# Bias rows moved in four pieces, first units multiplied by their high parts first, and the latent columns made in two lanes, in a two-block transformer kernel

## The reference, cut to what matters

```python
z = h @ w_in                                  # first block; h = rmsnorm(x, g[0])
bias = jnp.transpose(rel_bias_table[bucket], (2, 0, 1))        # one row of distances per head, 12 heads
scores = jnp.where(valid, scores + bias[None, None, :, None], NEG_INF)
...
proj = jnp.einsum('bsd,de->bse', h, w_in[l])  # second block
ya = swa_attention(...)                       # 8 heads, sliding window
yb = mla_attention(...)                       # 4 heads; q and kv from latent columns:
#   q  = rmsnorm_2(c_q)  @ w_uq               (384 -> 4 x (128 + 64))
#   kv = rmsnorm_2(c_kv) @ w_ukv              (256 -> 4 x (128 + 128))
yc = diff_attention(...)                      # 4 heads of two softmaxes; out = rmsnorm_2(out, subln_g) * (1 - lam_init)
x = x + jnp.einsum('bse,ed->bsd', y, w_out[l])
```

## Time and profile before

| | us |
|---|---|
| median of 3 runs (2353.87 to 2355.01) | 2354.45 |
| the profiled execution, its own time | 2355.84 |
| its span, from the first to the last instruction | 2354.1 |
| PE busy | 2253.3 (96%) |
| DVE busy | 1362.3 (58%) |
| ACT busy | 1067.9 (45%) |
| mean granted clock of TensorE | 0.979 of 2.4 GHz |

### The profile page before, as it was taken

One profiled execution on the slowest core, in us unless ns is written; L12 is line 12 of the kernel. 1 busy time (PEld: TensorE's weight loads), 2 busy tenths in 40 slices (PEclk: granted clock), 3 DMA queues, 4 the chain that ended last, 5 costly groups with the idle time before them and its releaser, 6 DMA issues.

```text
span 2354.1 us, 31707 instructions
## 1 busy us (share of the span) xinstructions
PE 2253.3 (96%) x12978; PEld 1959.9 (83%) x12978; DVE 1362.3 (58%) x1718; ACT 1067.9 (45%) x1376; POOL 62.9 (3%) x66
## 2 busy tenths in 40 slices
PE   8799999888989999999999999999999999999998
PEld 7788898787877888888888888888986889889776
DVE  5446666566556666767666444655445555544554
ACT  5343542424455544544555334545435443544443
POOL 0000101002000000000000000000000000000000
PEclk9899999899989999999999999999999999999999
DMA  7756440014634555555565555553550556445143
GB/s 279 189 191 202 163 158 1 1 32 154 203 118 134 190 185 188 186 187 187 186 206 191 190 192 196 185 195 120 181 178 19 180 178 222 159 152 174 59 129 140
DMA packets 237804, 375.59 MB, mean 160 GB/s; under 512 B 8535, under 2 KB 110072, under 8 KB 236920
## 3 DMA queue, kind: packets, MB, share of 16 engines
q1 hardware_dynamic: 229596, 362.83, 46.3%
q10 hardware_dynamic: 8092, 11.11, 1.9%
HBM read 369.45 MB, written 4.46 MB: 159 GB/s over the span
## 4 chain that ended last, share of the span: by engine, by line
PE 65%; issue 5%; DVE 4%; ACT 2%; POOL 0%; DVEq 0%; POOLq 0%; ACTq 0%
PE PS L482 16%; PE PS L441 12%; PE PS L443 12%; PE PS L442 12%; PE PS L485 8%; DVE w_lo L359 1%; PE PS L2062 1%; ACT w_hi L354 1%; PE PS L2152 1%; PE PS L2136 1%; PE PS L2046 1%; PE PS L2827 1%; DVE h_both L938 0%; PE PS L921 0%; ACT spare L2074 0%
## 5 line engine op out<-in xcount | busy, mean ns | idle before, releaser
L359 DVE TENSOR_TENSOR w_lo<-raw,w_hi 128x2048 fp32r<-128x2048 f32 (+2 forms) x340 | 766.8, 2256 | 765.2 <-ACT w_hi L354 765.0
L354 ACT ACTIVATE w_hi<-raw 128x2048 fp32r<-128x2048 f32 (+2 forms) x340 | 641.2, 1886 | 876.0 <-PE PS L443 494.4
L482 PE MATMUL PS<-h_both,w_hi 128*128 128x512 f32 x1968 | 541.6, 397 | 12.2 <-DVE w_lo L359 9.4
L441 PE MATMUL PS<-w_hi,h_both 128*128 128x512 f32 (+2 forms) x1344 | 514.9, 383 | 11.7 <-DVE h_both L943 4.5
L442 PE MATMUL PS<-w_lo,h_both 128*128 128x512 f32 (+2 forms) x1344 | 507.2, 377 | 0.0
L443 PE MATMUL PS<-w_hi,h_both 128*128 128x512 f32 (+2 forms) x1088 | 408.3, 375 | 0.0
L482 PEld LDWEIGHTS PS<-h_both,w_hi 128*128 128x128 f32 x1968 | 338.1, 190 | 59.4 <-ACT arena L609 9.6
L485 PEld LDWEIGHTS PS<-h_both,w_lo 128*128 128x128 f32 x1968 | 303.2, 189 | 42.2
L485 PE MATMUL PS<-h_both,w_lo 128*128 128x256 f32 x1968 | 314.0, 281 | 0.0
L441 PEld LDWEIGHTS PS<-w_hi,h_both 128*128 128x128 f32 x1344 | 254.3, 189 | 60.0 <-issue 6.0
L442 PEld LDWEIGHTS PS<-w_lo,h_both 128*128 128x128 f32 x1344 | 254.6, 189 | 45.4
(11 more groups left out here) (569 smaller groups left out, 2003.4 us busy)
## 6 DMA issues: line engine op xcount, KB each, us to landing
raw<-in_w_in SPq DMA_DIRECT2D x132, 1024.0 KB, 5.0
raw<-in_ffn_w_up SPq DMA_DIRECT2D x176, 512.0 KB, 4.3
raw<-in_w_out SPq DMA_DIRECT2D x48, 1024.0 KB, 5.1
raw<-in_ffn_w_down SPq DMA_DIRECT2D x44, 1024.0 KB, 5.0
raw<-in_mem_wkv SPq DMA_DIRECT2D x8, 1024.0 KB, 11.5
raw<-in_mem_wq SPq DMA_DIRECT2D x4, 1024.0 KB, 5.1
raw<-in_mem_wo SPq DMA_DIRECT2D x4, 1024.0 KB, 7.2
raw<-in_w_in SPq DMA_DIRECT2D x4, 768.0 KB, 4.6
```

The costliest lines, as they stand in the source:

```text
L354: act.activation(w_hi[:, slot % 2, :st.n], raw[:, slot, :st.n], ACT.Copy).then_inc(hi_made, 1)
L359: dve.tensor_tensor(w_lo[:, slot % 2, :st.n], raw[:, slot, :st.n], w_hi[:, slot % 2, :st.n].bitcast(F32), ALU.subtract).then_inc(lo_made, 1)
L441: pe.matmul(ps, l_hi, r_hi, start=start, stop=False, skip_group_check=skip)
L482: pe.matmul(sums, wh[:, k, cs], h_both[:, :, kk, :], start=kk == 0, stop=False, skip_group_check=True)
```

## The change

It has six edits. (1) `opening_tensor` turns two pairs, then multiplies unit 0 by a new function: block by block the products with `h_hi`, with pairs 2 and 3 turned in between, and then all the products with `h_lo`. ST_MEM_K keeps the old way. In the wide stages, unit 0 is then made of matmuls of 256 columns. (2) In the `unscaled_` openings, unit 1 of the weights is split ahead of pairs 2 and 3. (3) The bias rows go out in four pieces of three heads, after ST_C's units 0, 3, 6 and 9, and come back in four pieces beside the stages after ST_CE; no wait stands between ST_BC and ST_C. (4) The latent columns are two jobs of 7 rounds, on lanes 2 and 3; `mla` heads 2 and 3 idle for 7 rounds. (5) `mixed_scalar` splits `w_out_2`'s unit 0 three rounds earlier. (6) `mixed_vector` does its part of that ahead of `diff_rows`, a round earlier.

```diff
+        def multiply_highs_first(pe, q, hi_ready, lo_ready, turn):
...
+            pe.wait_ge(lo_made, q.unit(1))
...
+            for k in range(st.kb):
+                hi_ready(k)
+                for o, ts, ns, first in rows:
+                    pe.matmul(o, h_hi[:, k, ts], wh[:, k, ns], start=k == 0 and first, stop=False, skip_group_check=True)
+                    pe.matmul(o, h_hi[:, k, ts], wl[:, k, ns], start=False, stop=False, skip_group_check=True)
+                for o, _, cs, first in blocks:
+                    pe.matmul(o, wh[:, k, cs], h_hi[:, k, :], start=k == 0 and first, stop=False, skip_group_check=True)
+                    pe.matmul(o, wl[:, k, cs], h_hi[:, k, :], start=False, stop=False, skip_group_check=True)
+                turn(k)
+            for k in range(st.kb):
+                lo_ready(k)
+                for o, ts, ns, _ in rows:
+                    last = pe.matmul(o, h_lo[:, k, ts], wh[:, k, ns], start=False, stop=False, skip_group_check=True)
+                for _, o, cs, _ in blocks:
+                    last = pe.matmul(o, wh[:, k, cs], h_lo[:, k, :], start=False, stop=False, skip_group_check=True)
+            last.then_inc(unit_used, 1)
...
-        def opening_tensor(pe, st, j, block, ready=None):
-            for n in range(4):
+        def opening_tensor(pe, st, j, block, ready=None, highs_first=True):
+            for n in range(2):
                 turn_pair_tensor(pe, j, n, block, ready)
-            for u in range(4):
-                pe.wait_ge(j.dve, j[f"lo{4 * u + 3 if j.single else 2 * u + 1}"])
+            if highs_first:
+                multiply_highs_first(pe, Group(st, 0), lambda k: pe.wait_ge(j.act, j[f"hi{k}"]),
+                                     lambda k: pe.wait_ge(j.dve, j[f"lo{k}"]),
+                                     lambda k: turn_pair_tensor(pe, j, k + 2, block, ready) if k < 2 else None)
+            else:
+                for n in (2, 3):
+                    turn_pair_tensor(pe, j, n, block, ready)
+                pe.wait_ge(j.dve, j["lo3"])
+                multiply(pe, Group(st, 0), 0)
+            yield
+            for n in (4, 5):
+                turn_pair_tensor(pe, j, n, block, ready)
+            for u in range(1, 4):
+                pe.wait_ge(j.dve, j[f"lo{4 * u + 3}"])
                 multiply(pe, Group(st, 0), u)
                 yield
                 if u < 2:
...
             if not made:
                 split_hi(act, Group(st, 0), 0)
+            else:
+                split_hi(act, Group(st, 0), 1)
             for n in range(2, 4):
                 turn_pair_scalar(act, j, n, gain)
             yield
             for u in range(1, 4):
-                split_hi(act, Group(st, 0), u)
+                if u > 1 or not made:
+                    split_hi(act, Group(st, 0), u)
                 next(squares, None)
                 if u == 1:
...
             next(quarters, None)
+            if made:
+                split_lo(dve, Group(st, 0), 1)
             for n in range(2, 4):
...
-            latents = dict(kind="latents", name="latents", pe="q0 q1 k0 k1 v0 v1", act="q0c q1c k0c k1c", dve="v0c v1c")
-            jobs = [latents] + diff + mla
+            latents = [dict(kind="latents", name="latents", part=n, pe="q k v", act="qc kc", dve="vc") for n in range(2)]
...
-            for job in mla[1:]:
+            for job in mla[2:]:
                 job["idle"] = LATENT_ROUNDS
...
-            DIFF_, MLA = 1, 9
-            picks = [[DIFF_ + 0, DIFF_ + 4], [DIFF_ + 1, DIFF_ + 5], [0, MLA], [MLA + 1], [DIFF_ + 2, DIFF_ + 6],
+            DIFF_, MLA = 2, 10
+            picks = [[DIFF_ + 0, DIFF_ + 4], [DIFF_ + 1, DIFF_ + 5], [0, MLA], [1, MLA + 1], [DIFF_ + 2, DIFF_ + 6],
...
-        LATENT_ROUNDS = 13
+        LATENT_ROUNDS = 7
...
+            part, freed = j.job["part"], None
...
+                yield
+                if freed:
+                    pe.wait_ge(j.act, j[freed])
+                for hh in range(2):
+                    for k in range(n_k):
+                        h = 2 * part + hh
+                        last = pe.matmul(PS[:, bank, hh * S:(hh + 1) * S], wsrc[:, k, h * stride:h * stride + P], src[:, k, :],
+                                         start=k == 0, stop=k == n_k - 1)
                 last.then_inc(j.pe, 1)
-                yield
+                freed = f"{n}c"
+                yield
+            yield
+            pe.wait_ge(j.act, j["kc"])
+            for k in range(2):
+                last = pe.matmul(PS[:, bank, :], ckv_t[:, k, part * P:(part + 1) * P], ukv4[:, k, :, P:2 * P], start=k == 0,
+                                 stop=k == 1)
+            last.then_inc(j.pe, 1)
+            yield
...
+            for part in L2[layer]["latents"]:
+                j = part["steps"]
+                pe.wait_ge(j.act, j["kc"])
+                pe.wait_ge(j.dve, j["vc"])
...
-            yield from rounds(MIXED_SPLIT + 3)
+            yield from rounds(MIXED_SPLIT)
             free_lanes_made(act, layer)
             split_hi(act, Group(ST2[layer]["out"], 0), 0)
...
             dve.tensor_scalar(ssq, ssq, 1.0 / P, EPS, ALU.mult, ALU.add).then_inc(d.dve, 1)
             yield
-            yield
+            split_lo(dve, Group(ST2[layer]["out"], 0), 0)
             yield
             run(diff_rows(dve, layer))
-            split_lo(dve, Group(ST2[layer]["out"], 0), 0)
             yield
...
+        def bias_out(act):
+            for n in range(4):
+                hs = slice(3 * n, 3 * n + 3)
+                act.dma_start(shifted[hs], arena[hs, WROW:WROW + 384].unsqueeze(1).to_broadcast([3, P, 384]))\
+                   .then_inc(rel_out, 16)
+                yield
+                yield
+                yield
+
+        def bias_back(act):
+            for n in range(4):
+                act.dma_start(rel_bias[:, 3 * n:3 * n + 3, :],
+                              bass.AP(shifted.tensor, 3 * n * 384 * P + P - 1, [[383, P], [384 * P, 3], [1, S]]))\
+                   .then_inc(rel_back, 16)
+                yield
+                yield
+
...
-            run(products_tensor(pe, ST_MEM_K, opening_tensor(pe, ST_MEM_K, t_mem, blocks_of(mem_rows), mem_ready)))
+            run(products_tensor(pe, ST_MEM_K, opening_tensor(pe, ST_MEM_K, t_mem, blocks_of(mem_rows), mem_ready, False)))
...
-            act.dma_start(shifted, arena[0:A_H, WROW:WROW + 384].unsqueeze(1).to_broadcast([A_H, P, 384])).then_inc(rel_out, 16)
             run(products_scalar(act, ST_BC, more=True, opening=opening_scalar(act, ST_BC, t_x, gain_of("g_mix"))))
-            act.wait_ge(rel_out, 16)
-            act.dma_start(rel_bias, bass.AP(shifted.tensor, P - 1, [[383, P], [384 * P, A_H], [1, S]])).then_inc(rel_back, 16)
-            run(products_scalar(act, ST_C, before=end_of(ST_BC), more=True))
+            weave(products_scalar(act, ST_C, before=end_of(ST_BC), more=True), bias_out(act))
             run(products_scalar(act, ST_CE, before=end_of(ST_C), more=True))
-            act.wait_ge(rel_back, 16)
+            act.wait_ge(rel_out, 64)
...
-            fill = together(prepare_scalar(act), after(4, gating_scalar(act)), after(4, opened_scalar(act)))
+            fill = together(prepare_scalar(act), after(4, gating_scalar(act)), after(4, opened_scalar(act)), bias_back(act))
```

More of the change, by code:

```diff
@@ L496, in multiply @@
             last.then_inc(unit_used, 1)
+        def multiply_highs_first(pe, q, hi_ready, lo_ready, turn):
+            st, bank, slot = q.st, (2 * q.parity, 2 * q.parity + 1), q.first % 2
+            if st.G + q.c >= 2:
+                late = 0 if st.wide == 0 else -1
+                pe.wait_ge(act_evac, q.number(late))
+                pe.wait_ge(dve_evac, q.number(late))
+            pe.wait_ge(lo_made, q.unit(1))
+            wh = w_hi[:, slot, :st.n].rearrange("p (k n) -> p k n", k=st.kb)
+            wl = w_lo[:, slot, :st.n].rearrange("p (k n) -> p k n", k=st.kb)
+            at_once = bool(st.tok and st.ch)
+            rows, blocks = [], []
+            if st.tok:
+                c0, n = st.tok
+                rows = [(PS[:, bank[1], t * n:(t + 1) * n] if at_once else PS[:, bank[t], :n], slice(t * P, (t + 1) * P),
+                         slice(c0, c0 + n), not (at_once and t)) for t in range(TB)]
+            if st.ch:
+                c0, n = st.ch
+                for c in range(n // P):
+                    cs = slice(c0 + c * P, c0 + (c + 1) * P)
+                    if st.wide is None:
+                        o = PS[:, bank[c // 2], (c % 2) * S:(c % 2 + 1) * S]
+                        blocks.append((o, o, cs, c % 2 == 0))
+                    else:
+                        blocks.append((PS[:, q.bank + c, 0:S], PS[:, q.bank + c, S:2 * S], cs, True))
+            for k in range(st.kb):
[14 more added lines that the diff above has]
+            last.then_inc(unit_used, 1)
@@ L1015, in unscaled_opening_vector @@
             for u in range(1, 4):
-                split_lo(dve, Group(st, 0), u)
```

(8 more changed lines are left out.)

43 lines of the change are left out of this document (7 added, 36 removed).

## The result

The changed kernel takes 2321.64 us (median of 4 runs, 2318.35 to 2326.64) against 2354.16 us before (4 runs): a ratio of 0.9866, 95% interval 0.9845 to 0.9887, or 32.5 us less. The forecast of 2342.5 went the right way with about a third of the gain, and its range (from 2328) does not hold the result.

What follows compares the result with a forecast made beforehand. PE was taken as the bound, busy 96% of the span, leaving its idle time and half clock to gain. 12.4 - 12 + 2.0 + 1.3 + 0.4 + 7.8 = 11.9 us less gave 2342.5 us, range 2328 to 2362.

Steps and rivals of the forecast that it cites:

- The wait between ST_BC and ST_C: Between these stages, PE's 9.4 us wait goes and 3.0 us of half clock return: 12.4 us gained.
- The pieces: In ST_C, bias pieces make two weight loads 6.1 us late each: 12 us lost, bounds nothing and 47.
- The first rival: In ST_C, the bias pieces cost nothing: 23.9 us gained, 2330.5 us; chance 0.25.
- The slower rival: In ST_C, four pieces take 124 us and starve the weight loads, 47 us of stalls: 2377.6 us; chance 0.15.
- ST_BC's opening: At ST_BC's start, unit 0 can start about 2.2 us earlier: 2.0 us gained, bounds 0.7 and 2.4.
- Layer 1's q: At the opening of layer 1's q, PE's wait for h_lo goes: 1.3 us gained.
- The other three openings: In ST_MEM_Q, ST_UP and layer 0's q, work is swapped, not saved: 0.4 us gained for the three.
- The lanes: Per layer, 5.8 us of waits go, 1.7 of clock returns, new waits cost 2.8 and 0.8: 3.9 us gained.
- Untouched parts: In parts of the kernel that no edit touches, no change was forecast: 0 us.

Runs made afterwards that it cites:

- e8: The changed kernel with unit 0 multiplied in the old order in all six openings, all four pairs turned first; 2331.47 us.
- e5: The changed kernel with the bias rows sent out in one transfer of 12 rows after ST_C's unit 0, way back still in four pieces; 2329.4 us.
- e1: The kernel before with only the bias rows' change: out in four pieces during ST_C, back in four after ST_CE; 2339.31 us.
- e6: The changed kernel with the four bias pieces issued one right behind the other after ST_C's unit 0; 2356.37 us.
- e11: The changed kernel with a bias piece behind every second unit of ST_C in place of every third; 2333.79 us.
- e3: The kernel before with only the lanes' changes: latents in two lanes, w_out_2's unit 0 split earlier and ahead of diff's norm; 2342.34 us.
- e4: The kernel before with only the openings' changes: the new order for unit 0, and unit 1 split ahead of pairs 2 and 3; 2347.56 us.
- e7: The changed kernel with latents in two lanes, but w_out_2's unit 0 rounded three rounds later and its w_lo made behind diff's norm; 2335.63 us.
- e10: The changed kernel with the first pair's four transposes in ST_BC's opening issued five times in place of once; 2324.38 us.
- e12: The changed kernel with w_hi products first in w_out_2's units 0 and 1 and c_qk's unit 0, unit 0's w_lo made behind the mla outputs; 2311.73 us.

## Why the prediction was wrong

**The wait between ST_BC and ST_C (12.4): right.** e8 has ST_BC's old opening and the same stretch at half clock in it as the kernel before; from 8 to 24 it needs 97.9 us for 110.4, which is 12.5.

**The pieces (-12): the step that failed.** "A load that falls behind a piece as that one did is 24.2 - 18.1 = 6.1 us late" carried the landing time beside a transfer of 12 rows over to pieces of 3. e5 shows that size beside the whole (24.8 and 26.4, PE's wait 5.3); beside pieces it is 19.5 at most and falls, and PE's wait is zero (changed kernel, e1). The term was -12 and measured 0, its own lower bound. The first rival, free pieces, was the case, and at 0.25 it had too little. Its 2330.5 is still 8.9 us above the result: the lanes and the untouched parts make up that difference.

**The slower rival.** Its premise, that a row alone goes no faster than twelve together, is false: 79 us for the four pieces, not 124, and 83 ns a packet on average, not 225. The three engines were right: each piece has three completions in the trace. By the estimate from the Trainium skill's page "SBUF — State Buffer", section "Door 1: The DMA port swizzle", the pieces were to take some 24, 16, 16 and 24 us. Those numbers come from the row's 74 GB/s over three ports, 24.7 each; with the 27.2 that the prediction quotes from the page they would be 22, 14, 14 and 22. The first packet began at 91, the 384th, 768th and 1152nd at 112, 130 and 147, and the last at 169, so the quarters took 22, 18, 17 and 22. There the page was nearer than the sum from the row. But there was a slower case, through a mechanism that I did not consider: ACT's issue held by its own queue (e6, e11). "ACT's queue issues 6 more transfers; ACT is 45% busy in all" costed it at nothing, and the spacing made that true.

**ST_BC's opening (2.0): a sum that came out by luck.** PE in the changed kernel:

```profile
65.81 0.35 PE L526 MATMUL PS<-w_hi,h_both 128*128 128x256 f32 x1 [1.40 <-ACT h_both L970]
```

Unit 0 starts at 65.81 for 67.25, in a trace that is 0.5 us later there, so 2.0 us earlier, as said. But 0.9 us of that are the transposes of pairs 2 and 3, which only moved, and unit 1 now waits 0.44: of idle time 2.50 - 1.40 - 0.44 = 0.7 us is gained, my lower bound. The rest is half clock: from 67 to 73 the granted clock was 0.72 in before and in e8, 1.00 in the changed kernel, and 1.00 too in e1 and e3, which have the old opening. So it can't be put down to the edit. **Layer 1's q (1.3):** 1.0. **The other three openings (0.4):** 1.8, of which about 1.4 in layer 0's q. There half clock lasts 6.8 us before and 3.4 now; e1 and e3, with the old opening and 3.4 us of it, need 31.7 and 31.6 us for 31.2, so 0.5 is the edit's.

**The lanes (3.9 a layer): right mechanism, mis-sized term.** Idle time of PE went from 6.7 to 3.6 us in the stretch, 3.1 less, for a forecast 5.8 - 2.8 = 3.0. Half the lost clock was booked as coming back, 1.7; all 3.4 us of it did, and PE's busy time fell by 4.2, 0.8 more than the clock explains. Unit 1 lost 0.4, not 0.8. In all 6.8 for 3.9. Here the clock goes with the edit: the kernels with the old lanes (before, e1, e4) have two stretches at half clock in the lanes of each layer, and none with the new lanes has one there; e7 and e8 have one in layer 0 at w_out_2's first matmuls, behind PE's wait.

**Untouched parts (0): missed.** 5.5 us of half clock in the mixer and in both layers' token products, which no edit touches; what decides where it falls stays open (e10). No row of before could have given its sign; it belonged into the range, as some 5 us on either side, and the low end would then have been 2323, still 1.4 above the median.

## What to carry to other kernels

Don't price a transfer by what a four times larger one did beside the same loads: in pieces the same bytes left PE without a wait, the worst load 1 us past its slack (e1), whole they did not (e5). Leave room between large transfers that an engine issues which also computes, since its stream can stop at the issue itself (e6, e11). Before a gain of some us is put down to an edit, look whether the granted clock changed in parts that no edit touches (e10). When a stage is made to end sooner, move with it what the next one needs (edit 4 without 5 and 6 gave 1 us of 7 a layer), or order the products so that the late operand comes last (e12).

## What was not expected of the hardware

ACT's issue of a transfer of 384 packets of 1536 bytes took 0.7 us when the one before was nearly through, and 8.7 to 18.1 us when more than about one and a half such transfers were left (e6, e11). The same packets took 225 ns with twelve rows at once and mostly 65 ns with three; over the whole transfer their mean fell from 204 to 83 ns. With the same instructions one execution had a stretch at half clock where another had none (before and e3), and from `w_lo` 24 to 72 the kernels needed 473.6 to 478.6 us. Why the first two loads beside the pieces land latest, and the next eight each 0.2 to 2.2 us sooner, was not tried.
